# Scores of two steps between the token blocks of a value panel, and a batch of modulation weights loaded before two panels

## The chip, the cores and the metric

The kernel runs on one core of a Trainium2 chip. The core has five engines, each with its own instruction queue, which meet only through semaphores: TensorE (PE, matmuls; its weight loads are shown as PEld), VectorE (DVE), ScalarE (ACT), GpSimd (POOL) and SyncE (SP, which here only issues loads). The metric is the device time of one execution in microseconds (us). All arithmetic is in float32; large products are made from a high and a low part of each operand, in three matmuls.

## The reference

Four layers of a transformer on 512 tokens of width 1024, two with modulation by a vector c, two without. Cut to what the change touches:

```python
def layer_ab(x, c, ...):                      # layer 0
    sh_m, sc_m, g_m, sh_f, sc_f, g_f = jnp.split(silu(c) @ mod_w + mod_b, 6)
    h = rmsnorm(x, norm_mix) * (1.0 + sc_m) + sh_m
    (a_gate, a_x, q, kc, vc, ks, vs, kw, vw, gts) = _split(h @ w_in, IN0_SIZES)
    y_a = rg_lru(causal_conv(a_x), ...) * gelu(a_gate)
    y_b = nsa_mixer(q, kc, vc, ks, vs, kw, vw, sigmoid(gts), ...)   # attention, run 0
    x = x + g_m * (concatenate([y_a, y_b]) @ w_out)
    ...
# layer 1: dsa_mixer (attention over the best 128 keys, run 1)
# layer 2: no softmax attention
# layer 3:
    q, k, v = rotary(qkv[0]), rotary(qkv[1]), qkv[2]
    o = dilated_attention(q, k, v)            # run 2
# in each run, for every head and block of 128 queries:
    s = q @ k.T * scale;  p = softmax(where(mask, s, -inf));  o = p @ v
```

## The kernel before

**Panels.** Weights come from memory as 378 panels of 1024 x 128 (0.5 MB), through a ring of four slots (RING). SP loads a panel into `raw` (L553), ACT rounds it to its high part `w_hi` (split_hi, L1197), POOL subtracts to get the low part `w_lo` (split_lo, L597), and PE multiplies (L662 to L664), into PSUM bank p % 4 for panel p. ACT or DVE then copies the bank away, which counts `bank_free` up. A slot is split anew when PE is done with it. Two panels of values at a time are done by token_panels instead: tokens are the rows of the output then, in QB = 4 blocks of 128 tokens, 24 matmuls of 256 columns each; DVE copies the result out (copy_tokens, L1583 or L1586).

**Modulation.** The first sixteen columns of the modulation come as four batches of 2 MB (`first_mods`, load_first, L562). SP's queue is: columns, x, batch 0, panels 0 to 2, batches 1 to 3, panel 3, then the rest. Of a batch DVE sums three quarters by weight (sum_first, L1858 and L1865) and PE does one quarter and the sums over partitions (first_batch, L672 and L676). first_h(n) on DVE then makes blocks 2n and 2n+1 of h (L1950 to L1965), for which it needs the norm's root: ACT squares x, POOL and PE add, ACT splits panels 0 to 2 and only then takes the root (L1342), DVE takes its reciprocal (invert_root, L1604) in the middle of batch 1's sum, PE spreads it over a bank (spread, L784). PE's panels 0 to 2 run over blocks 0 to 3 of h, then wait for blocks 4 to 7.

**Attention.** Each of the three runs has N_PAIR = 32 steps; a step is a block i of 128 queries and a pair of heads (b = 0, 1), and blocks alternate, 512 keys, 128 keys, 512, 128 and so on at first. Step n goes: scores on PE into two banks (L837), mask and minimum on DVE (masked, L1773), exponentials and sums on ACT (L1283), the reciprocal on DVE (invert, L1783; in run 0 times a gate, L1788), the weights on POOL (weights, L614), transposes on PE (turn, L847), copies to SBUF on ACT and DVE, values on PE (L866). PE issues scores up to SCORES_AHEAD = 3 steps ahead. Steps 0 (banks 4 and 5) differ from the others, which go round banks 0, 1, 6 (run 0) or 0, 1, 6, 7. From n = 2 on, scores wait for `masked_ready` of the step that last had the bank.

Runs 0 and 2 are EARLY: their scores 0 are issued ahead of the last value panel (last_panels: in run 0 panels P_VS, P_VW = 16, 17; in run 2 the panels before P_OUT3), and masks, exponentials, inverse and weights of step 0 are placed beside that panel in the other engines' queues. In run 0 scores 0 stand behind a wait for the key of the windows (kwT, L1364), which ACT copies late because of the recurrence's decays (lru_decays). DVE, behind the token copy of run 0, does two products of the recurrence (recurrence_gated, L2010, two inputs in SBUF), in steps 0 and 1 of its attention loop; POOL splits panels 20 and 21 in the same time.

The order of everything is that in which the code is written, per engine; no scheduler moves it.

Of the kernel before, what the change touches and what calls it, by code (L numbers as in the profile page):

```python
# [131 lines left out]
def build(nc, A):  # L132
    with ExitStack() as ctx:
# [356 lines left out]
        EARLY = (0, 2)  # L490
# [46 lines left out]
        SCORE_BANKS = ((0, 1, 6), (0, 1, 6, 7), (0, 1, 6, 7))  # L537
        PROB_SLOT = (0, 2, 3, 1)

        def score_bank(run, n, b):  # L540

            own = SCORE_BANKS[run]
            return bank[4 + b] if n == 0 else bank[own[(2 * n + b - 2) % len(own)]]
# [4 lines left out]
        def _(sp_):  # L548
# [18 lines left out]
            for p in range(3):  # L567
                load_raw(p)
            for n in range(1, BATCHES):
                load_first(n)  # L570
# [22 lines left out]
        def _(pool):  # L593
# [23 lines left out]
            def attention(run):  # L617

                for n in range(1 if run in EARLY else 0, N_PAIR):
                    weights(run, n)  # L620
                    if run == 0 and n in (8, 9, 10, 11):
                        recurrence_low(n - 8)
# [11 lines left out]
            weights(0, 0)  # L634
            split_from(P_OUT0 + 2, 2)
# [17 lines left out]
            weights(2, 0)  # L653
            split_from(P_OUT3 + 2, 2)
# [5 lines left out]
        def _(pe):  # L660
# [56 lines left out]
            def token_panels(p):  # L717
# [11 lines left out]
                m.then_inc(panel_done, 2)  # L729
# [98 lines left out]
            def attention(run, p_out, last_panels=None):  # L828
                pairs_, at = (PAIRS0, PAIRS1, PAIRS1)[run], N_PAIR * run

                def scores(n):

                    if n >= 2:
# [51 lines left out]
                scores(0)  # L885
                if last_panels is not None:
                    last_panels()
                for n in range(1, SCORES_AHEAD):
# [134 lines left out]
            def last_panels():  # L1023
                token_panels(P_VS)
# [4 lines left out]
            pe.wait_ge(bank_free, P_VS)  # L1029
            pe.wait_ge(cpt_copied, 2)  # L1030
# [143 lines left out]
            def last_panels():  # L1174
                token_panels(P_OUT3 - 2)
# [10 lines left out]
        def _(act):  # L1186
# [99 lines left out]
            def attention(run):  # L1286
# [26 lines left out]
                for n in range(N_PAIR):  # L1313
                    if n >= SCORES_AHEAD:
                        copy_even(n - SCORES_AHEAD)
                    if n or run not in EARLY:
# [75 lines left out]
            for p in range(P_OUT0):  # L1392
# [35 lines left out]
                if p == P_VS:  # L1428
                    exponentials(0, 0)
                split_hi(p + RING)  # L1430
# [117 lines left out]
            for p in range(P_V3, P_OUT3):  # L1548
                if p == P_OUT3 - 2:
                    exponentials(2, 0)  # L1550
                split_hi(p + RING)
# [12 lines left out]
        def _(dve):  # L1564
# [226 lines left out]
            def attention(run, beside=None, times=0):  # L1791
# [20 lines left out]
                early = 1 if run in EARLY else 0  # L1812
# [158 lines left out]
            sum_first(1, lambda: invert_root(0))  # L1971
# [117 lines left out]
            for p in range(P_OUT0):  # L2089
# [22 lines left out]
                elif p == P_VW:  # L2112
                    invert(0, 0)
                    dve.wait_ge(bank_free, P_VS)
# [259 lines left out]
            for p in range(P_V3 + 2, P_OUT3, 2):  # L2374
                if p == P_OUT3 - 2:
                    masked(2, 0, 0)
                    masked(2, 0, 1)
                    invert(2, 0)
                copy_tokens(p, v3t, P * (p - P_V3), root[:, QB:2 * QB])
# [146 lines left out]
```

## Time and profile before

| | us |
|---|---|
| three timed runs | 2465.38, 2467.26, 2467.51 (median 2467.26) |
| the profiled execution | 2463.97 |
| its span on the core | 2462.2 |
| PE busy | 2385.1, 97% of the span |
| DVE, ACT, POOL busy | 1299.1 (53%), 944.3 (38%), 1083.4 (44%) |
| PE's waits in all at L837 (scores) for masks | 9.6, three times |

The profile is of one execution. Its rows give the start of an instruction or of a merged group from the span's start, its duration, and in brackets how long its engine had been idle and who ended that. PE is the engine that is busy nearly always, so its idle stretches are what there is to win. A busy PE isn't always at its peak: its granted clock has two levels, 1.00 (2.4 GHz) and 0.50 (1.2 GHz), and the same matmul takes about twice as long at the lower one.

### The profile page before, as it was taken

What the parts mean: (1) busy time and instruction counts of PE and PEld (TensorE: products, weight loads), DVE (VectorE), ACT (ScalarE), POOL (GpSimd) and SP (SyncE); (2) the same over time, 40 slices, a digit from 0 to 9 for tenths busy, and PEclk for the clock granted to TensorE, in tenths of its full rate; (3) what the DMA queues carried; (4) which work ended last, traced back from release to release, by engine and by line L of the source; (5) the groups of instructions that cost most, each with busy time, mean ns of one, the idle gap of its engine ahead of it and who ended that gap; (6) DMA issues with size and microseconds to landing.
All of it is one profiled execution on the core that took longest, in us unless ns stands there. A gap on an engine that the chain in (4) does not pass through costs nothing.

```text
span 2462.2 us, 34882 instructions
## 1 busy us (share of the span) xinstructions
PE 2385.1 (97%) x11957; PEld 1932.4 (78%) x11957; DVE 1299.1 (53%) x2334; ACT 944.3 (38%) x1538; POOL 1083.4 (44%) x513
## 2 busy tenths in 40 slices
PE   7989999999999899999999989999999999999998
PEld 6776778888876577888888768888888967888887
DVE  6777554443248753111137976455467564645455
ACT  3458332222333743322234544322246374422222
POOL 2336334344433543443445834444454454344433
PEclk9999989999999899999999999999999999999999
DMA  7531335554222012222222213222232201232222
GB/s 309 193 129 53 129 137 180 195 176 146 104 79 78 26 69 82 97 95 94 102 94 94 70 66 121 103 86 103 94 112 97 94 24 60 86 106 92 101 94 77
DMA packets 64195, 261.52 MB, mean 106 GB/s; under 512 B 7248, under 2 KB 7760, under 8 KB 57936
## 3 DMA queue, kind: packets, MB, share of 16 engines
q1 hardware_dynamic: 61056, 251.00, 28.5%
q10 hardware_dynamic: 3024, 8.98, 1.0%
q8 instruction: 73, 1.20, 0.2%
q14 instruction: 42, 0.34, 0.0%
HBM read 257.86 MB, written 2.10 MB: 106 GB/s over the span
## 4 chain that ended last, share of the span: by engine, by line
PE 83%; DVE 7%; issue 4%; POOL 1%; DVEq 1%; DMA 1%; ACT 1%; POOLq 1%; SPq 0%; ACTq 0%
PE bank L662 25%; PE bank L664 25%; PE bank L663 25%; PE bank L847 2%; PE bank L837 2%; PE bank L866 2%; POOL w_lo L597 1%; DVE acc L1596 1%; DVE top L2172 1%; DVEq L2175 1%; DMA first_mods<-in_first 1%; DVE bank L1865 1%; POOLq L651 1%; DVE bank L2222 1%; DVE iacc L2161 1%
## 5 line engine op out<-in xcount | busy, mean ns | idle before, releaser
L597 POOL TENSOR_TENSOR w_lo<-raw,w_hi 128x1024 fp32r<-128x1024 f32 x378 | 917.1, 2434 | 1243.8 <-ACT w_hi L1197 1242.4
L662 PE MATMUL bank<-h_hi,w_hi 128*128 128x512 f32 x1760 | 697.8, 396 | 12.8 <-DVE h_lo L1643 7.8
L664 PE MATMUL bank<-h_hi,w_lo 128*128 128x512 f32 x1760 | 690.3, 392 | 0.0
L663 PE MATMUL bank<-h_lo,w_hi 128*128 128x512 f32 x1760 | 690.2, 392 | 0.0
L1197 ACT ACTIVATE w_hi<-raw 128x1024 fp32r<-128x1024 f32 x378 | 392.5, 1051 | 431.9 <-PE bank L664 428.9
L662 PE MATMUL bank<-g_hi,w_hi 128*128 128x512 f32 x1072 | 418.5, 390 | 0.0
L664 PE MATMUL bank<-g_hi,w_lo 128*128 128x512 f32 x1072 | 417.2, 389 | 0.0
L663 PE MATMUL bank<-g_lo,w_hi 128*128 128x512 f32 x1072 | 417.1, 389 | 0.0
L662 PEld LDWEIGHTS bank<-h_hi,w_hi 128*128 128x128 f32 x1760 | 333.9, 190 | 90.5 <-DVE h_lo L1643 8.7
L664 PEld LDWEIGHTS bank<-h_hi,w_lo 128*128 128x128 f32 x1760 | 333.5, 189 | 71.1
L663 PEld LDWEIGHTS bank<-h_lo,w_hi 128*128 128x128 f32 x1760 | 334.2, 190 | 68.6 <-issue 0.5
L664 PEld LDWEIGHTS bank<-g_hi,w_lo 128*128 128x128 f32 x1072 | 201.2, 188 | 42.3
L662 PEld LDWEIGHTS bank<-g_hi,w_hi 128*128 128x128 f32 x1072 | 201.2, 188 | 41.6 <-issue 0.2
L663 PEld LDWEIGHTS bank<-g_lo,w_hi 128*128 128x128 f32 x1072 | 201.3, 188 | 41.4
L1733 DVE TENSOR_TENSOR prod<-silu,bank 128x512 f32<-128x512 f32 x44 | 30.3, 688 | 303.1 <-PE bank L664 302.8
L614 POOL TENSOR_TENSOR prob<-prob,stat 128x1024 f32<-128x1024 f32 (+1 forms) x96 | 120.1, 1254 | 94.6 <-DVE stat L1783 57.2
L1262 ACT ACTIVATE g_hi<-prod 128x512 f32 x66 | 41.7, 633 | 300.3 <-DVE prod L1733 197.3
L1659 DVE SCALAR_TENSOR_TENSOR x<-bank,plain,x 128x512 f32<-128x512 f32 x64 | 47.6, 748 | 156.9 <-PE bank L664 156.8
L1865 DVE SCALAR_TENSOR_TENSOR bank<-modraw,csil,bank 128x256 f32<-128x256 f32 x222 | 108.5, 489 | 16.9 <-issue 0.4
L1283 ACT ACTIVATE prob<-prob,stat 128x512 f32<-128x512 f32 (+1 forms) x192 | 106.7, 558 | 24.0 <-DVE stat L1773 23.4
L1659 DVE SCALAR_TENSOR_TENSOR x<-bank,modv,x 128x512 f32<-128x512 f32 x64 | 47.3, 748 | 119.2 <-PE bank L664 118.3
L1773 DVE CUSTOM_DVE_ANT_0 prob<-bank,mask 128x512 f32<-128x512 f32 (+1 forms) x192 | 90.1, 485 | 30.7 <-PE bank L837 27.2
(296 smaller groups left out, 2525.0 us busy)
## 6 DMA issues: line engine op xcount, KB each, us to landing
raw<-in_panels SPq DMA_DIRECT2D x378, 512.0 KB, 3.4
modraw<-in_pairs SPq DMA_DIRECT2D x40, 1024.0 KB, 5.6
first_mods<-in_first SPq DMA_DIRECT2D x4, 2048.0 KB, 22.0
x<-in_x SPq DMA_DIRECT2D x1, 2048.0 KB, 8.2
w<-in_w ACTq DMA_DIRECT2D x1, 2048.0 KB, 8.4
out<-yout ACTq DMA_DIRECT2D x8, 256.0 KB, 2.2
mask<-in_causal ACTq DMA_DIRECT2D x1, 1024.0 KB, 5.0
mask<-in_dilated ACTq DMA_DIRECT2D x1, 1024.0 KB, 7.1
```

The costliest lines, as they stand in the source:

```text
L597: pool.tensor_tensor(w_lo[:, slot, :], raw[:, slot, :], w_hi[:, slot, :].bitcast(F32), ALU.subtract)\
L614: pool.tensor_tensor(both, both, stat[:, 2, u:u + 2].rearrange("p (b o) -> p b o", o=1) .broadcast_to((P, 2, w)), ALU.mult).then_inc(weigh ...
L662: pe.matmul(out, w_h, m_h, start=start, stop=False)
L663: pe.matmul(out, w_h, m_l, start=False, stop=False)
L664: return pe.matmul(out, w_l, m_h, start=False, stop=stop)
L837: pe.matmul(score_bank(run, n, b)[:, 0:w], q_of(run, pairs_[n], b), k_of(run, pairs_[n], b), start=True, stop=True).then_inc(score_ready, 1)
L847: m = pe.transpose(bank[2 + b][:, P * j:P * j + P], prob[:, PROB_SLOT[n % PROB_STEPS], b, P * j:P * j + P], ident[:, :])
L1197: act.activation(w_hi[:, slot, :], raw[:, slot, :], ACT.Copy).then_inc(hi_ready, 1)
L1283: act.activation(row, row, ACT.Exp, bias=stat[:, 0, u % 64:u % 64 + 1], scale=-1.0, accum_out=stat[:, 1, u % 64:u % 64 + 1]).then_inc(exp_ ...
L1659: dve.scalar_tensor_tensor(out=x[:, n, :], in0=bank[p % RING][:, :], scalar=scale_by, in1=x[:, n, :], op0=MUL, op1=ADD).then_inc(bank_free, 1)
L1773: dve.tensor_tensor_reduce(row_of(n, b, w), score_bank(run, n, b)[:, 0:w], mask[:, i, 0:w], -SCALE, HIGHEST, ADD, ALU.min, stat[:, 0, u % ...
L1865: m = dve.scalar_tensor_tensor(out=part if k < KB - 1 else to, in0=w[:, :, k, :], scalar=csil[:, k:k + 1], in1=part, op0=MUL, op1=ADD)
```

## The change

- SP's queue at the start: columns, x, batch 0, panel 0, batch 1, panels 1 and 2, batches 2 and 3, panel 3.
- DVE takes the reciprocal of the first root before it begins batch 1's sum; it stood in the middle of that sum.
- In runs 0 and 2 token_panels takes a function `beside`, called behind each of the four blocks of tokens of the last value panel: behind block 0 it issues scores 0, behind block 2 scores 1. The waits for the key and for run 0's cpT move from before the attention into scores 0.
- Scores 1 use banks 4 and 5 as scores 0 do, in all three runs, and wait for both masks of step 0. Steps from 2 on have the banks that they had; scores 2 no longer wait for a mask.
- DVE, ACT and POOL treat step 1 of runs 0 and 2 as step 0 was treated: mask, exponentials, inverse and weights stand ahead of the token copy (DVE), of the split of panel 20 (ACT) and of the splits of panels 20 and 21 (POOL); in run 2 likewise.

```diff
-        EARLY = (0, 2)
+        EARLY = (2, 0, 2)
...
-        SCORE_BANKS = ((0, 1, 6), (0, 1, 6, 7), (0, 1, 6, 7))
+        SCORE_BANKS = ((6, 0, 1), (6, 7, 0, 1), (6, 7, 0, 1))
...
-            return bank[4 + b] if n == 0 else bank[own[(2 * n + b - 2) % len(own)]]
+            return bank[4 + b] if n < 2 else bank[own[(2 * n + b - 4) % len(own)]]
...
             load_first(0)
-            for p in range(3):
+            load_raw(0)
+            load_first(1)
+            for p in range(1, 3):
                 load_raw(p)
-            for n in range(1, BATCHES):
+            for n in range(2, BATCHES):
                 load_first(n)
...
             weights(0, 0)
+            weights(0, 1)
             split_from(P_OUT0 + 2, 2)
...
-            def token_panels(p):
+            def token_panels(p, beside=None):
...
-                m.then_inc(panel_done, 2)
+                    if j == QB - 1:
+                        m.then_inc(panel_done, 2)
+                    if beside is not None:
+                        beside(j)
...
                 def scores(n):
 
-                    if n >= 2:
+                    if run == 0 and n == 0:
+                        pe.wait_ge(bank_free, P_VS)
+                        pe.wait_ge(cpt_copied, 2)
+                    if n == 1:
+                        pe.wait_ge(masked_ready, 2 * at + 2)
+                    elif n >= 3:
                         pe.wait_ge(masked_ready, 2 * (at + n) + 2 - len(SCORE_BANKS[run]))
...
-                scores(0)
                 if last_panels is not None:
-                    last_panels()
-                for n in range(1, SCORES_AHEAD):
+                    last_panels(lambda j: scores(j // 2) if j in (0, 2) else None)
+                for n in range(EARLY[run], SCORES_AHEAD):
                     scores(n)
...
                 if p == P_VS:
                     exponentials(0, 0)
+                    exponentials(0, 1)
...
             sum_first(0)
-            sum_first(1, lambda: invert_root(0))
+            invert_root(0)
+            sum_first(1)
             first_h(0)
...
                 elif p == P_VW:
+                    dve.drain()
+                    for b in range(2):
+                        masked(0, 1, b)
                     invert(0, 0)
+                    invert(0, 1)
                     dve.wait_ge(bank_free, P_VS)
                     copy_tokens(P_VS, vtok0, 0)
```

The same lines for run 2 (weights, exponentials, masks, inverse) are left out.

VectorE at the start, in the order of its queue, before (bank is where the running sum lies, first_mods_80 is batch 1, the row with x3 stands for three instructions):

```order
L1865 SCALAR_TENSOR_TENSOR modsum<-first_mods_79,csil,bank 128x384
L1858 TENSOR_SCALAR bank<-first_mods_80,csil 128x384
L1865 SCALAR_TENSOR_TENSOR bank<-first_mods_80,csil,bank 128x384 x3
L1604 RECIPROCAL root<-root 128x4
L1865 SCALAR_TENSOR_TENSOR bank<-first_mods_80,csil,bank 128x384 x3
L1865 SCALAR_TENSOR_TENSOR modsum<-first_mods_80,csil,bank 128x384
L1950 TENSOR_TENSOR modv<-bank,cols 128x2x2
```

and after:

```order
L1876 SCALAR_TENSOR_TENSOR modsum<-first_mods_79,csil,bank 128x384
L1615 RECIPROCAL root<-root 128x4
L1869 TENSOR_SCALAR bank<-first_mods_80,csil 128x384
L1876 SCALAR_TENSOR_TENSOR bank<-first_mods_80,csil,bank 128x384 x6
L1876 SCALAR_TENSOR_TENSOR modsum<-first_mods_80,csil,bank 128x384
L1961 TENSOR_TENSOR modv<-bank,cols 128x2x2
```

The reciprocal moved from between the fourth and fifth of batch 1's eight instructions to ahead of all of them.

VectorE at the entry of run 0, before (ya is the product of recurrence_gated, L1773 the masks with the bank that they read, vtok the token copy):

```order
L2010 TENSOR_TENSOR ya_97<-ya_97,xc_109 128x512 x2
L1783 RECIPROCAL stat_69<-stat_69 128x2
L1788 TENSOR_TENSOR stat_69<-stat_69,small_76 128x2
L1583 COPY vtok0_107<-bank0 128x512
L1583 COPY vtok0_107<-bank1 128x512
L1843 TENSOR_TENSOR modv_60<-bank7,cols_57 128x20
L2010 TENSOR_TENSOR ya_97<-ya_97,xc_109 128x512
L1773 ISA prob_94,stat_69<-bank0,mask_66 128x128
L1773 ISA stat_69 128x1
L1773 ISA prob_94,stat_69<-bank1,mask_66 128x128
L1773 ISA stat_69 128x1
L2010 TENSOR_TENSOR ya_97<-ya_97,xc_109 128x512
```

and after:

```order
L1784 ISA prob_94,stat_69<-bank4,mask_66 128x128
L1784 ISA stat_69 128x1
L1784 ISA prob_94,stat_69<-bank5,mask_66 128x128
L1784 ISA stat_69 128x1
L1794 RECIPROCAL stat_69<-stat_69 128x2
L1799 TENSOR_TENSOR stat_69<-stat_69,small_76 128x2
L1794 RECIPROCAL stat_69<-stat_69 128x2
L1799 TENSOR_TENSOR stat_69<-stat_69,small_76 128x2
L1594 COPY vtok0_107<-bank0 128x512
L1594 COPY vtok0_107<-bank1 128x512
L1854 TENSOR_TENSOR modv_60<-bank7,cols_57 128x20
L2022 TENSOR_TENSOR ya_97<-ya_97,xc_109 128x512 x2
```

The masks of step 1 and its inverse moved from between and behind the two products to ahead of the token copy, behind the products of chunks 2 and 3; the two products that follow the copy now stand side by side.

TensorE at the same place, before:

```order
L664 MATMUL bank<-w_hi,h_lo 128x256
L683 MATMUL bank<-ones,modsum 128x1 x2
L837 MATMUL bank<-ksT,q_98 128x128 x2
L837 MATMUL bank<-kwT,q_98 128x512 x2
L837 MATMUL bank<-kwT,q_98 128x128 x2
L847 MATMUL bank<-ident,prob 128x128 x8
```

and after:

```order
L668 MATMUL bank<-w_hi,h_lo 128x256
L849 MATMUL bank<-ksT,q_98 128x128 x2
L666 MATMUL bank<-w_hi,h_hi 128x256
...
L668 MATMUL bank<-w_hi,h_lo 128x256
L687 MATMUL bank<-ones,modsum 128x1 x2
L849 MATMUL bank<-kwT,q_98 128x512 x2
L849 MATMUL bank<-kwT,q_98 128x128 x2
L859 MATMUL bank<-ident,prob 128x128 x8
```

Scores 1 (ksT, 128 columns) moved from behind the value panel to ahead of its fourth block.

## Rows read from the trace of the kernel before

**Rows 1.** Order of time, ACT at the start: start us, us, instruction, [idle before, releaser].

```profile
16.98 1.06 ACT L1197 ACTIVATE w_hi<-raw 128x1024 fp32r<-128x1024 f32 x1 [0.23 <-DMA raw<-in_panels]
18.24 1.06 ACT L1197 ACTIVATE w_hi<-raw 128x1024 fp32r<-128x1024 f32 x1 [0.21 <-DMA raw<-in_panels]
...
20.68 0.29 ACT L1342 ACTIVATE root<-bank 128x1 f32<-128x1 f32 x3
```

**Rows 2.** Order of time, DVE at the start.

```profile
23.14 0.62 DVE L1858 TENSOR_SCALAR bank<-first_mods,csil 128x384 f32<-128x384 f32 x1 [3.12 <-DMA first_mods<-in_first]
...
25.76 0.17 DVE L1604 RECIPROCAL root<-root 128x4 f32<-128x4 f32 x1
...
32.58 0.16 DVE L1950 TENSOR_TENSOR modv<-bank,cols 128x4 f32<-128x4 f32 x1 [0.30 <-PE bank L676]
```

**Rows 3.** Order of time, PE at the start, panel 0 taken up again.

```profile
50.16 0.79 PE L662 MATMUL bank<-h_hi,w_hi 128*128 128x512 f32 x1 [1.87 <-DVE h_lo L1965]
```

**Rows 4.** Stretches: from:to, length, PE busy, granted clock, DMA share, GB/s.

```profile
61.00:162.80 101.80, 101.75 (x524) 78.75 (x523) 74.95 (x131) 45.25 (x58) 36.14 (x15) 1.00 0.49 181
...
190.70:191.90 1.20, 1.20 (x8) 0.61 0.00 0
...
820.60:823.10 2.50, 2.50 (x21) 0.50 0.00 0
```

**Rows 5.** Order of time, PE at the entry of run 0.

```profile
165.52 1.13 PE L837 MATMUL bank<-ksT,q 64*128 64x512 f32 x4 [2.77 <-ACT kwT L1364]
...
178.19 0.50 PE L683 MATMUL bank<-ones,modsum 128*128 128x1 f32 x4
179.80 0.49 PE L837 MATMUL bank<-ksT,q 64*128 64x128 f32 x4 [1.11 <-DVE vtok L1583]
182.88 2.08 PE L837 MATMUL bank<-kwT,q 64*128 64x512 f32 x4 [2.59 <-DVE stat L1773]
186.03 0.80 PE L837 MATMUL bank<-kwT,q 64*128 64x128 f32 x4 [1.07 <-DVE stat L1773]
```

**Rows 6.** Order of time, DVE at the entry of run 0.

```profile
176.00 1.48 DVE L2010 TENSOR_TENSOR ya<-ya,xc 128x512 f32<-128x512 f32 x2
...
178.46 1.29 DVE L1583 COPY vtok<-bank 128x512 f32<-128x512 f32 x2 [0.67 <-PE bank L664]
...
180.44 2.17 DVE L2010 TENSOR_TENSOR ya<-ya,xc 128x512 f32<-128x512 f32 x1 [0.61 <-issue]
...
183.12 2.24 DVE L2010 TENSOR_TENSOR ya<-ya,xc 128x512 f32<-128x512 f32 x1
185.29 0.68 DVE L1773 CUSTOM_DVE_ANT_0 prob<-bank,mask 128x512 f32<-128x512 f32 x1
```

**Rows 7.** Order of time, ACT, the last of step 1's exponentials in run 0.

```profile
183.61 0.19 ACT L1283 ACTIVATION_READ_ACCUMULATOR prob<-prob,stat 128x1 f32 x1
```

**Rows 8.** Order of time, POOL at the entry of run 0.

```profile
177.87 1.89 POOL L614 TENSOR_TENSOR prob<-prob,stat 128x1024 f32<-128x1024 f32 x1 [8.98 <-DVE stat L1788]
179.72 2.34 POOL L597 TENSOR_TENSOR w_lo<-raw,w_hi 128x1024 fp32r<-128x1024 f32 x1
182.02 2.80 POOL L597 TENSOR_TENSOR w_lo<-raw,w_hi 128x1024 fp32r<-128x1024 f32 x1
186.98 0.61 POOL L614 TENSOR_TENSOR prob<-prob,stat 128x256 f32<-128x256 f32 x1 [2.16 <-DVE stat L1788]
```

**Rows 9.** Order of time, PE at the entry of run 1.

```profile
813.55 2.50 PE L837 MATMUL bank<-k,q 64*128 64x512 f32 x8 [5.92 <-DVE stat L1773]
816.67 1.97 PE L847 MATMUL bank<-ident,prob 128*128 128x128 f32 x8 [0.61 <-POOL prob L614]
```

**Rows 10.** Order of time, DVE at the entry of run 1, the inverse of step 0.

```profile
814.48 0.17 DVE L1783 RECIPROCAL stat<-stat 128x2 f32<-128x2 f32 x1 [0.55 <-ACT prob L1283]
```

**Rows 11.** Order of time, PE at the entry of run 2.

```profile
1976.02 1.58 PE L837 MATMUL bank<-k,q 64*128 64x128 f32 x12 [1.38 <-DVE v3t L1586]
...
1981.17 0.44 PE L847 MATMUL bank<-ident,prob 128*128 128x128 f32 x2 [1.28 <-POOL prob L614]
```

More of the change, by code:

```diff
@@ L617, in attention @@
             def attention(run):
-                for n in range(1 if run in EARLY else 0, N_PAIR):
+                for n in range(EARLY[run], N_PAIR):
                     weights(run, n)
@@ L653, in _ @@
             weights(2, 0)
+            weights(2, 1)
             split_from(P_OUT3 + 2, 2)
@@ L1022, in _, with last_panels @@
                     compressed_turned()
-            def last_panels():
-                token_panels(P_VS)
+            def last_panels(beside):
+                token_panels(P_VS, beside)
                 with_mods(P_VS)
@@ L1027, in last_panels @@
                 pe.wait_ge(bank_free, P_OUT0)
-            pe.wait_ge(bank_free, P_VS)
-            pe.wait_ge(cpt_copied, 2)
             attention(0, P_OUT0, last_panels)
@@ L1172, in _, with last_panels @@
                 token_panels(p)
-            def last_panels():
-                token_panels(P_OUT3 - 2)
+            def last_panels(beside):
+                token_panels(P_OUT3 - 2, beside)
                 pe.wait_ge(bank_free, P_OUT3)
@@ L1315, in attention @@
                         copy_even(n - SCORES_AHEAD)
-                    if n or run not in EARLY:
+                    if n >= EARLY[run]:
                         exponentials(run, n)
@@ L1550, in _ @@
                     exponentials(2, 0)
+                    exponentials(2, 1)
                 split_hi(p + RING)
@@ L1810, in out_low @@
                                       out_block(run, n, to_hi).bitcast(F32), SUB).then_inc(ot_lo, 1)
-                early = 1 if run in EARLY else 0
+                early = EARLY[run]
                 for n in range(N_PAIR):
@@ L2375, in _ @@
                 if p == P_OUT3 - 2:
-                    masked(2, 0, 0)
-                    masked(2, 0, 1)
+                    for n in range(2):
+                        for b in range(2):
+                            masked(2, n, b)
                     invert(2, 0)
+                    invert(2, 1)
                 copy_tokens(p, v3t, P * (p - P_V3), root[:, QB:2 * QB])
```

## Prediction

> **What bounds the kernel now.** The page says that TensorE (PE) is busy nearly throughout, so an edit pays only if it shortens a stretch in which PE waits, and it costs if it makes a new one. The diff touches four such places: the start, and the entry of each of the three attentions (runs 0, 1, 2). I then read the waits of PE and, engine by engine, the order of time around each place.
>
> At the start PE's panel 0 stops half way and waits 1.87 us for h_lo from VectorE (DVE) [rows 3]. DVE has no slack there: it waits 3.12 us for the second modulation batch, takes it up at 23.14, and from then on is idle only 0.30 us [rows 2] until it releases PE at 50.16. Behind the start, from 61.0 to 162.8, PE is busy for 101.75 of 101.80 us [rows 4]. So a shift of DVE at the start becomes a shift of everything, one for one.
>
> At the entry of run 0 PE waits four times: 2.77, 1.11, 2.59 and 1.07 us [rows 5]. Run 1 has one wait, 5.92 us for the first masked scores, and 0.61 us for the first weights [rows 9]. Run 2 has 1.38 us for the copy of the value panel and 1.28 us for weights from GpSimd (POOL) [rows 11].
>
> **Part 1, the start.** The batch is put ahead of panels 1 and 2 on SP's queue, and DVE takes the reciprocal of the first root before the second batch's sum, no longer in its middle. Bytes in order: before, panel 2 landed at 18.24 and the batch behind it (2 MB) at 23.14, so 4.9 us for 2 MB and 1.2 us for a panel of 0.5 MB [rows 1, 2]. Now the batch lands near 18.24 - 2 x 1.2 + 4.9 = 20.7, and panel 2 near 23.1, since the same bytes come in ahead of it. DVE would be free for the batch at 20.02, so this alone would bring 2.4 us. But the reciprocal now stands in front of the sum, and it needs the root. ScalarE (ACT) makes the root behind its split of panel 2: the split, a table load and four roots, in all from 18.24 to 20.97 [rows 1], 2.7 us. With panel 2 at 23.1 the root is done at 25.85, the reciprocal at 26.05, and the sum starts at 26.1 instead of 23.14: 2.96 later. The sum is free of the reciprocal, which took a slot of 0.1 to 0.2 in its middle, and the idle 0.30 us is swallowed [rows 2], which leaves **+2.6 us**, for h_lo and so for PE. PE has room meanwhile: its 1.87 us of waiting stays about as long. Bounds: 0 if panels 1 and 2 still landed by 18.24; +2.9 if the 0.30 isn't swallowed.
>
> **Part 2, run 0.** PE now begins the value panel at once (162.75), and scores 0 come behind its first block of tokens. From 166.6 to 178.2 the four blocks take 11.6 us [rows 5], 2.9 each, so scores 0 stand at 165.65, when their key (the wait that ended at 165.52) is ready. The 2.77 us are hidden. Scores 1 come after the third block, and PE is through at 176.2 instead of 178.7. What is late next is DVE, not PE:
> - Up to 177.4, where its gated products of chunks 2 and 3 end [rows 6], DVE goes as before (scores 0 end within 0.15 us of where they did).
> - Now it masks scores 1, 0.5 us (182.61 to 183.12 in [rows 6]), and inverts step 0 (0.4 us, what lies between 177.4 and the 0.67 of idling at 178.46), so POOL gets its factor at 178.45 rather than 177.87 [rows 8]. ACT's exponentials of step 1 end 1.2 us after the mask started ([rows 6, 7]: 182.6 to 183.80), at 178.75. DVE waits for them, inverts step 1 (0.4) and copies the tokens from 179.25 instead of 178.46 [rows 6].
> - PE's next scores waited until 1.34 us after that copy began [rows 5, 6]: now 180.6. PE is idle for 4.4 us, and scores 2 run from 180.6.
> - POOL does the weights of step 0 (1.85), now those of step 1 too (0.6), and then splits two panels; the split starts at 178.45 + 1.85 + 0.6 = 180.9 instead of 179.72 [rows 8].
> - DVE reaches the two gated products (L2010) at 181.2, and they fall under those splits again.
>
> How those products behave decides the sum. Alone, 1.48 us for two would be 0.7 each [rows 6]; under the splits they show 2.17 and 2.24. The first ended 0.6 us after the first split (which ended at 182.0), and the second split took 2.80 and ended at 184.82, the second product 0.5 us later [rows 6, 8]. They stand until a split is over. So the second product ends 0.5 us after the second split, and that is 1.2 us later than before: masks of scores 2 at 186.5 instead of 185.29, scores 3 at 187.25 instead of 186.03, **+1.2 us**; the rest of the run follows in the same order. The Trainium skill states this too ("SBUF — State Buffer", section "SBUF: two separate sides": a VectorE instruction with two SBUF inputs and a GpSimd instruction that reads SBUF lock each other out for a whole instruction); the trace agrees, by the 0.5 us. Were the two merely slowed, each at its 2.2 us, the masks would stand at 185.75 and the term would be +0.5.
>
> Bounds: +0.5, and +2 if the token copy, which ran beside POOL's weights in 1.29 [rows 6, 8], were held by them; a case below gives less than zero.
>
> **Part 3, run 1.** It has no value panel to lie beside, but the table of banks changes for it too: scores 1 now use the banks of scores 0 and wait until both are masked. In the row of 813.55, scores 2 and 3 went out together [rows 9]; now scores 1, 2 and 3 go out there. Masks 1 wait for scores 1, whose two halves take 0.8 us at this clock (scores 3 at 186.03 in [rows 5] are the same shape), so the inverse that stood at 814.48 [rows 10] moves to 814.75, and the first transposes from 816.67 to 817.0: **+0.3 us**. Bounds: +0.7 (all of the 0.8 shows), and -1.5, if PE, now without its 0.61 us of idling, gets the high clock back earlier than at 823.1 [rows 4].
>
> **Part 4, run 2.** PE has one step of scores (0.4 us) less behind the panel and one more ahead of it; it waits for the token copy either way, and scores 2 stand where they did. Weights 1 are made ahead of the two splits, so the 1.28 us at 1981.17 go [rows 11]. But weights 2 now stand behind the same splits: those start 0.4 later (the panel ends 0.4 later) and 0.6 of weights is gone from behind them. So transposes 2 come 0.2 earlier than before: **-0.2 us**. Bounds: -1.3 and +0.4.
>
> Wait tests and a few drains are the rest: no row shows one over 0.1 us.
>
> **The sum:** 2.6 + 1.2 + 0.3 - 0.2 = +3.9 us. The profiled execution took 2463.97 us, so it would take 2467.9. The timed runs stand at a median of 2467.26 (3.3 above it), so I forecast 2471.2, by +3.9 from that median.
>
> **Rivals.**
> - *The loads land out of order.* If panels 1 and 2 come in beside the batch, the root is there at 21 as before, and the batch not before 23.1. Then the start gives 0 and the sum is +1.3: 2468.6. For it: all share 16 engines. Against: panels 1 and 2 landed 1.26 us apart, and the batch, four times as large, 4.9 us behind them [rows 1, 2]. The Trainium skill ("DMA: Bandwidth & Descriptors", "Queues, rings and completion order") says that completion isn't strictly first in, first out per issuing engine; the rows here look like it is. 8%.
> - *The early batch pays.* The sum starts at 20.7 and the reciprocal costs nothing: -2.4 at the start, -1.1 in all, 2466.2. Against it stands ACT's order, in which the root is behind panel 2. 4%.
> - *A product slips in ahead of the split.* In run 0 DVE asks at 181.2 and POOL at 180.9. If DVE is 0.3 us sooner, the first product takes 0.7, only one split stands before the second, and the masks stand at 184.8: -0.5 instead of +1.2; in all +2.2, 2469.5. 14%.
> - *Slower: the low clock stays longer in run 0.* Behind the wait at 182.88 scores of one size took 2.08 us, against 1.13 at 165.52 [rows 5]: the clock was at its lower level, 0.50 or 1.2 GHz, and came back inside 190.7 to 191.9 [rows 4], 5.4 us after PE took up work at 186.03. In run 1 it took from 813.55 to behind 823.1, 9.6 us, with one gap of 0.61 us [rows 4, 9]. After the change PE idles for 4.4 us, works for 2 and idles for 4.5 more. If the return takes 9.6 us from 187.25, there are 4.2 us more at half speed, 2.1 us lost: +6.0, 2473.3. It decides from a return after 194.7. 14%.
>
> **How the numbers follow.** The forecast has 60%, the rivals 8, 4, 14 and 14. About 0.2%, 4.9 us, is what a measurement of this kernel can tell from no change. The forecast's own terms reach from about +2.5 to +5, and the runs before spread over 2.1 us, so I put 12 of its 60 above +4.9; with the clock's 14 that makes 26% slower. Faster by 4.9 us has no case, 2% for what I don't see; 72% within. The range 2466.5 to 2474.0 takes in every case but the second rival's lower part, with a margin for the spread of the runs.
>
> **What would show it.** Start: the second sum's first row on DVE at 26.1 behind the reciprocal (at 20.7 the second rival, at 23.1 the first), panel 2's split on ACT at 23.1, PE's panel 0 resumed at 52.8. Run 0, times less the shift of 2.6: no wait of PE before scores 0, token copy at 179.25, split at 180.9, scores 3 at 187.25, clock back near 192.6. Run 1: PE's transposes 0.3 us later. Run 2: no wait for weights 1, one of 1.3 us for weights 2. I am wrong if the root isn't last at the start, or if the three entries together differ from +1.3 by more than 1.5 us.

## The result and the profile after

| | before | changed |
|---|---|---|
| median of the timed runs (lowest to highest), us | 2465.53 (2462.84 to 2467.51), 12 runs | 2470.04 (2465.75 to 2471.18), 12 runs |
| ratio to before | | 1.0016, interval 1.0008 to 1.0023 |
| the profiled execution, us | 2463.97 | 2466.16 |
| its span, us | 2462.2 | 2464.4 |

The change costs 0.16%, 3.9 us by the ratio and 4.5 by the medians: slower, and just inside what was called no change. The forecast was +3.9.

The two profiled executions are only 2.2 us apart. Executions of one kernel differ, much of it by how much of the time TensorE was granted its high clock: over the span, the mean clock goes from 0.981 to 0.985. With one straight line for all kernels of this study, an execution is 1.2 us shorter for each 0.001 of mean granted clock, and single executions then scatter by 0.7 us around their kernel's line. The profiled execution of the changed kernel was one of two at 0.985; five of the twelve were at 0.981, with a mean of 2470.9. The profiled execution of before was at 0.985 too, so the mean clock doesn't explain the small difference of the pair: by the line they would be 3.6 us apart, and before's lies 1.0 us above the line while the other's lies 0.4 us below it, which is within the scatter. At an equal clock the change costs 3.6 us; the twelve executions of before that were timed beside it have no clock on record, so this figure rests on the 93 timed later. The table of experiments below gives it for each kernel too, worked out in the same way.

**The start, after.** ACT's order of time (start us, us, instruction, idle before and releaser), to be held beside [rows 1]:

```profile
15.94 1.06 ACT L1206 ACTIVATE w_hi<-raw 128x1024 fp32r<-128x1024 f32 x1 [1.93 <-DMA raw<-in_panels]
22.12 1.06 ACT L1206 ACTIVATE w_hi<-raw 128x1024 fp32r<-128x1024 f32 x1 [5.12 <-DMA raw<-in_panels]
23.39 1.06 ACT L1206 ACTIVATE w_hi<-raw 128x1024 fp32r<-128x1024 f32 x1 [0.21 <-DMA raw<-in_panels]
24.46 1.28 ACT L1351 ACT_TABLE_LOAD   x1
...
25.82 0.29 ACT L1351 ACTIVATE root<-bank 128x1 f32<-128x1 f32 x3
```

Panels 1 and 2 land behind the batch, at 22.12 and 23.39, and the root is made behind both splits. DVE's order of time, beside [rows 2]:

```profile
26.15 0.18 DVE L1615 RECIPROCAL root<-root 128x4 f32<-128x4 f32 x1 [5.89 <-ACT root L1351]
26.25 0.59 DVE L1869 TENSOR_SCALAR bank<-first_mods,csil 128x384 f32<-128x384 f32 x1
27.35 4.11 DVE L1876 SCALAR_TENSOR_TENSOR bank<-first_mods,csil,bank 128x384 f32<-128x384 f32 x6 [0.51 <-issue]
...
35.79 0.16 DVE L1961 TENSOR_TENSOR modv<-bank,cols 128x4 f32<-128x4 f32 x1
```

DVE idles 5.89 us for the root where it had idled 3.12 for the batch, and begins the sum at 26.25. PE, beside [rows 3], takes up panel 0 at 53.37 and not at 50.16, with the whole start 0.24 us later from the first batch on (14.74 against 14.50):

```profile
53.37 0.80 PE L666 MATMUL bank<-h_hi,w_hi 128*128 128x512 f32 x1 [1.45 <-DVE h_lo L1976]
```

**Run 0, after.** The shift of the start is in these times: it stands at +2.7 us here. The 0.5 us between this and the 3.21 at panel 0 came back by the clock: it was low around the resumed panel and rose 4.9 us after it in before (50.16 to about 55.0) and 3.8 us after it here (53.37 to about 57.2). PE, beside [rows 5]:

```profile
168.37 1.13 PE L849 MATMUL bank<-ksT,q 64*128 64x512 f32 x4
...
175.38 0.49 PE L849 MATMUL bank<-ksT,q 64*128 64x128 f32 x4
...
184.39 2.08 PE L849 MATMUL bank<-kwT,q 64*128 64x512 f32 x4 [5.13 <-DVE vtok L1594]
190.09 0.80 PE L849 MATMUL bank<-kwT,q 64*128 64x128 f32 x4 [3.62 <-DVE stat L1784]
```

Scores 0 and 1 lie between the token blocks, with no wait: the 2.77 us are gone. Two waits of 5.13 and 3.62 us stand in the place of 1.11, 2.59 and 1.07. DVE and POOL, beside [rows 6] and [rows 8]:

```profile
180.99 0.16 DVE L1799 TENSOR_TENSOR stat<-stat,small 128x2 f32<-128x2 f32 x1
181.57 0.17 DVE L1794 RECIPROCAL stat<-stat 128x2 f32<-128x2 f32 x1 [0.42 <-ACT prob L1292]
181.81 1.33 DVE L1799 TENSOR_TENSOR stat<-stat,small 128x2 f32<-128x2 f32 x1
183.06 1.28 DVE L1594 COPY vtok<-bank 128x512 f32<-128x512 f32 x2
...
184.56 4.86 DVE L2022 TENSOR_TENSOR ya<-ya,xc 128x512 f32<-128x512 f32 x2
189.35 0.68 DVE L1784 CUSTOM_DVE_ANT_0 prob<-bank,mask 128x512 f32<-128x512 f32 x1
```

```profile
181.23 2.60 POOL L616 TENSOR_TENSOR prob<-prob,stat 128x1024 f32<-128x1024 f32 x2 [9.62 <-DVE stat L1799]
183.79 5.09 POOL L599 TENSOR_TENSOR w_lo<-raw,w_hi 128x1024 fp32r<-128x1024 f32 x2
```

The stretch in which the clock came back, at 193.7:

```profile
193.00:194.00 1.00, 1.00 (x4) 0.22 (x3) 0.00 (x0) 1.00 (x5) 1.00 (x1) 0.66 0.00 0
```

POOL's two splits end at 188.88 and DVE's two gated products 0.5 us later, as they did before. One thing is new: the little product of step 1's inverse (128x2), 0.16 us for step 0, takes 1.33 us for step 1. It began beside POOL's weights of step 0.

**Runs 1 and 2, after.** PE, beside [rows 9] and [rows 11]:

```profile
815.29 2.93 PE L849 MATMUL bank<-k,q 64*128 64x128 f32 x12 [5.89 <-DVE stat L1784]
818.74 1.09 PE L859 MATMUL bank<-ident,prob 128*128 128x128 f32 x8 [0.51 <-POOL prob L616]
...
1977.80 1.35 PE L849 MATMUL bank<-k,q 64*128 64x512 f32 x8 [1.38 <-DVE v3t L1597]
...
1981.98 0.41 PE L859 MATMUL bank<-ident,prob 128*128 128x128 f32 x2 [0.53 <-ACT probT L1304]
...
1984.24 1.09 PE L859 MATMUL bank<-ident,prob 128*128 128x128 f32 x8 [0.41 <-POOL prob L616]
```

The first transposes of run 1 take 1.09 us at once and not 1.97: here the clock was already back. The profile's stretches show it (columns as in [rows 4], after PE the other engines):

```profile
817.00:818.40 1.40, 1.23 (x6) 0.42 (x4) 1.09 (x4) 0.34 (x2) 1.40 (x1) 0.53 0.00 0
818.40:820.30 1.90, 1.56 (x11) 1.16 (x12) 1.71 (x9) 1.74 (x5) 0.90 (x2) 1.00 0.00 0
```

Before, it came back at 823.1 [rows 4]. This took the profiled execution from +2.1 us at these transposes to -0.1 at the run's last ones. Later it fell back again, to +1.2 ahead of run 2 and +2.2 at the end, so it is one of several such swings in this pair and not a gain that stayed.

### The profile page after: what moved, and what is told of

Its sections match the earlier page's. It is cut to its first block, busy times and chain, and to the rows that moved or that the text cites. A ratio compares the mean times of both kernels' runs of the same rounds, so it can differ in the third digit from the quotient of the medians.

```text
span 2464.4 us, 34883 instructions
## 1 busy us (share of the span) xinstructions
PE 2384.8 (97%) x11957; PEld 1932.7 (78%) x11957; DVE 1301.8 (53%) x2334; ACT 942.9 (38%) x1538; POOL 1082.9 (44%) x513
## 4 chain that ended last, share of the span: by engine, by line
PE 84%; DVE 7%; issue 3%; DVEq 2%; POOL 1%; ACT 1%; DMA 1%; POOLq 1%; SPq 0%; ACTq 0%
PE bank L666 25%; PE bank L668 25%; PE bank L667 25%; PE bank L849 2%; PE bank L859 2%; PE bank L878 2%; DVEq L2191 1%; DVE top L2188 1%; POOL w_lo L599 1%; DMA raw<-in_panels 1%; DVE acc L1607 1%; POOLq L654 1%; DVE bank L2238 1%; DVE iacc L2177 1%; DVE bank L1876 1%
```

## The experiments

Theory: three of the change's four places cost what the sum says; the start is the dear one, since the root moved behind the batch and the reciprocal stands in front of the sum; in run 0 POOL's splits hold DVE's gated products. Rival for the start: the loads alone do it. Rival for run 0: the products are slow by themselves, or hiding the wait pays. Rival for run 1: it gives back 2 us by its clock, as the profiled execution looks.

Each kernel was timed against before on the same chip. "Equal clock" is the difference to before by the line described above (93 executions of before, 11 of each other, 12 of the changed kernel). The line has two limits. It takes out what an edit does to the clock itself, so where that is the question (q0, r1) the ratio is what counts; and the executions of before, taken by round, lie up to 0.4 us apart on it, so a figure is good to about 0.4 us. The last two columns are read in each profiled execution, less before's: PE's panel 0 taken up again (50.16 before), and by how much the shift grows over run 0, from the end of the stretch ahead of it (162.75 before) to the first matmul of the projection behind it (258.02 before). They are those of one execution, clock and all.

| kernel | median us | ratio (interval) | equal clock | PE at 50.16 | run 0 |
|---|---|---|---|---|---|
| changed | 2470.04 | 1.0016 (1.0008 to 1.0023) | +3.6 | +3.21 | +0.5 |
| s1, the start alone | 2467.85 | 1.0010 (1.0001 to 1.0019) | +2.5 | +2.94 | -0.1 |
| s2, the loads alone | 2467.23 | 1.0002 (0.9993 to 1.0011) | +0.3 | +0.19 | +1.7 |
| s3, start with the root ahead | 2463.17 | 0.9989 (0.9980 to 0.9998) | -2.3 | -1.81 | +3.0 |
| a1, the three entries alone | 2466.03 | 1.0001 (0.9991 to 1.0010) | +0.6 | -0.14 | +1.0 |
| q0, run 0's entry alone | 2464.44 | 0.9999 (0.9990 to 1.0008) | -0.1 | +0.12 | +0.9 |
| r1, run 1's entry alone | 2466.20 | 1.0005 (0.9996 to 1.0014) | +0.4 | +0.07 | +1.5 |
| r3, before with products ahead | 2462.42 | 0.9991 (0.9982 to 1.0000) | -1.8 | -0.29 | -1.4 |
| r2, a1 with products ahead | 2464.88 | 0.9998 (0.9989 to 1.0007) | +0.4 | -0.14 | -0.2 |
| best1, changed, root and products ahead | 2463.57 | 0.9995 (0.9986 to 1.0004) | -1.3 | -1.60 | -0.1 |
| best2, before with start, root, products ahead | 2461.53 | 0.9985 (0.9976 to 0.9994) | -3.4 | -1.98 | -0.7 |
| best3, best1 with inverse 1 behind the copy | 2460.53 | 0.9985 (0.9976 to 0.9994) | -3.2 | -1.89 | -1.3 |

### The start: s1, s2, s3

s2 is before with the new order of loads alone; s1 has the reciprocal ahead of the sum too; s3 is s1 with ACT's root ahead of its splits. The three edits:

```
             load_first(0)
-            for p in range(3):
+            load_raw(0)
+            load_first(1)
+            for p in range(1, 3):
                 load_raw(p)
...
-            sum_first(1, lambda: invert_root(0))
+            invert_root(0)
+            sum_first(1)
...
-            for p in range(3):
-                split_hi(p)
+            split_hi(0)
             act.wait_ge(sums_ready, 1)
             for j in range(QB):
                 m = act.activation(root[:, j:j + 1], ...)
             m.then_inc(root_ready, 1)
+            for p in range(1, 3):
+                split_hi(p)
```

> The kernel before with the new load order and the reciprocal ahead of the sum, the attentions as before. Theory (the reciprocal waits for a root that is made behind panel 2): the second sum starts on DVE near 26.1, PE takes panel 0 up again 2.6 to 3 us later than at 50.16, and PE's marks near 76, 105 and 142 stand 2.7 later, as in the changed kernel: time +2.7 us. Rival (most of the change's loss is made in the attentions, and the start is absorbed later): marks back to +0 by 300, time within 1 us.

> The kernel before with the new load order only; the reciprocal stays in the middle of the sum. Theory: the sum starts near 20.7, stands still in its middle until the root at 25.9, and ends at 28.8 as before (28.7): PE's marks within 0.3 us, time within 0.5 us. Rival (it is the later landing of panels 1 and 2, not the reciprocal's place, that costs): +2 us or more.

> The new load order, the reciprocal ahead of the sum, and ACT's root ahead of its splits of panels 1 and 2, so that the root waits for no load behind panel 0. Theory: root near 21, the sum starts near 21.1 instead of 23.14, PE's marks stand 1.9 us earlier, time -1.9 us. Rival (DVE would be late for another reason, such as PE's part of batch 1): 0 to -0.5.

s1 shows the change's start, +2.9 at PE and +2.5 at an equal clock. In s2 the batch lands at 20.63 and DVE takes it up at once, but half way it meets the reciprocal and waits for the root (DVE, order of time):

```profile
20.63 0.62 DVE L1860 TENSOR_SCALAR bank<-first_mods,csil 128x384 f32<-128x384 f32 x1 [0.57 <-DMA first_mods<-in_first]
21.33 2.02 DVE L1867 SCALAR_TENSOR_TENSOR bank<-first_mods,csil,bank 128x384 f32<-128x384 f32 x3
25.94 0.18 DVE L1606 RECIPROCAL root<-root 128x4 f32<-128x4 f32 x1 [2.59 <-ACT root L1344]
26.21 2.01 DVE L1867 SCALAR_TENSOR_TENSOR bank<-first_mods,csil,bank 128x384 f32<-128x384 f32 x3
```

Half of the sum lies in the wait, and s2 comes out level with before. So the late root bounds both, and where the reciprocal stands decides whether the sum's first half is beside it or behind it. In s3 ACT makes the root before it waits for panel 1, and DVE gets all (first ACT, then DVE):

```profile
19.08 0.36 ACT L1343 ACTIVATE root<-bank 128x1 f32<-128x1 f32 x4 [1.10 <-PE bank L913]
21.81 1.06 ACT L1199 ACTIVATE w_hi<-raw 128x1024 fp32r<-128x1024 f32 x1 [2.37 <-DMA raw<-in_panels]
```

```profile
20.05 0.18 DVE L1607 RECIPROCAL root<-root 128x4 f32<-128x4 f32 x1
20.53 0.62 DVE L1861 TENSOR_SCALAR bank<-first_mods,csil 128x384 f32<-128x384 f32 x1 [0.30 <-DMA first_mods<-in_first]
```

The sum starts at 20.53, PE's panel 0 is taken up 1.8 us earlier than before and 5.0 earlier than in the changed kernel, and the kernel is faster than before by 0.11%. The sum starts 2.6 us earlier than before and PE only 1.8. Lost on the way are 0.51 us in a gap behind the sum's first instruction, and 0.64 at a little product behind the sum (gains, 128x2, two inputs in SBUF), which takes 0.80 us at 26.82 where it took 0.16 in before, and ends at 27.62 with POOL's two splits (22.95 to 27.61); the reciprocal's slot in the sum and the idle 0.30 us are saved. The early load was a good edit with one order left as it was.

### Run 0 and run 1 alone: a1, q0, r1

a1 is the changed kernel with the first two of these edits taken back. q0 is a1 with runs 1 and 2 as before; r1 is before with the banks and the wait of run 1 alone. q0 against the changed kernel (the start, the waits and run 2's lines, which go back to before, are left out), then r1 against before:

```
-        EARLY = (2, 0, 2)
+        EARLY = (2, 0, 1)
...
-        SCORE_BANKS = ((6, 0, 1), (6, 7, 0, 1), (6, 7, 0, 1))
+        SCORE_BANKS = ((6, 0, 1), (0, 1, 6, 7), (0, 1, 6, 7))
...
+            first = 2 if run == 0 else 1
+            return bank[4 + b] if n < first else bank[own[(2 * (n - first) + b) % len(own)]]
```

```
-            return bank[4 + b] if n == 0 else bank[own[(2 * n + b - 2) % len(own)]]
+            return bank[4 + b] if n < (2 if run == 1 else 1) else bank[own[...]]
...
-                    if n >= 2:
+                    if n == 1 and run == 1:
+                        pe.wait_ge(masked_ready, 2 * at + 2)
+                    elif n >= (3 if run == 1 else 2):
```

> The changed kernel with the start as before. Theory: +1.3 us by the forecast's terms (run 0 +1.2, run 1 +0.3, run 2 -0.2); by the trace of the changed kernel run 0 +0.5, run 2 0 to -0.1, and run 1 anything from +0.3 to -2.5 as the clock comes back late or early; time between -2 and +1.3. Rival (the entries are what costs): +3 us or more.

> Before, with the entry of run 0 alone as in the change (start, run 1 and run 2 as before). My theory of the trace of the change: PE's wait of 2.77 us before scores 0 is gone, yet scores 3 come later than their 186.03 of before, because DVE copies the tokens later and the two gated products still stand until POOL's second split is over; the recorded sum has +1.2 us for it, and the trace of the change gave +1.4 at scores 3 (190.09, less the start's 2.7). So: split near 181.1, scores 3 near 187.4, whole kernel +1.2 us (2 at most). A theory in which hiding the wait pays gives -1 us or less. The look at the entries alone gave +1.64 at the first transposes and +1.25 from the third on.

> Before, with run 1's banks and wait alone as in the change. The recorded term is +0.3 us at the first transposes (from 816.67), since scores 1 go out behind the first masks and not ahead of them; bounds +0.7 and -1.5, the latter if PE has the high clock back sooner. The trace of the change lost nothing and won 2.2 us here (from +1.98 to -0.09), because the clock rose at 818.4 and not at 823.0. If the edit does that, this kernel shows the same, and it is some 2 us faster than before; if the moment at which the clock rises wanders by itself, transposes stand 0 to 0.3 us later and the time is within 0.5 us of before.

The entries together cost 0.6 us at an equal clock, and no interval tells them from nothing. In run 0 a1 and q0 show what the changed kernel shows: the copy late, DVE's products of 4.86 us under the splits, and a shift that grows by 0.9 to 1.0 us. But the timed q0 is at -0.2 us by its ratio, with an interval from -2.5 to +2.0, and at -0.1 at an equal clock. A possible reason is in the profiled executions of the kernels that keep the wait of 2.77 us before scores 0. In before, s1 and best2 the four matmuls behind it took 1.13 us, and from there to the small matmuls at the panel's end it was 12.7 us. In four others the clock fell about this wait. PE in s3:

```profile
163.87 2.08 PE L839 MATMUL bank<-ksT,q 64*128 64x512 f32 x4 [2.77 <-ACT kwT L1367]
```

and its stretches:

```profile
164.00:166.00 2.00, 2.00 (x5) 0.50 (x5) 0.00 (x0) 1.98 (x2) 1.16 (x1) 0.50 0.88 274
166.00:168.00 2.00, 2.00 (x10) 2.00 (x11) 1.81 (x5) 1.99 (x5) 1.20 (x1) 0.50 0.60 250
168.00:170.00 2.00, 2.00 (x12) 2.00 (x12) 1.77 (x5) 1.97 (x3) 0.00 (x0) 0.58 0.84 252
170.00:172.00 2.00, 2.00 (x19) 2.00 (x18) 1.83 (x4) 1.10 (x4) 0.00 (x0) 1.00 0.03 10
```

There the same piece took 15.3 us (s3, r1), 15.4 (s2) and 14.2 (r3). In the six kernels whose scores lie between the blocks the clock stayed at 1.00 throughout. So the wait cost, beside its 2.77 us, 1.5 to 2.7 us in four executions of seven, and the profiled execution of before, on which the forecast rests, was one of the three without. Taking the wait away gives that back where it happens. How often it happens in timed runs no row shows; that it evens out run 0's loss there fits q0's ratio, whose interval holds +0.9 just as well, so it isn't shown. The equal clock can't tell here: it takes such a gain out.

In r1 the first transposes come 3.45 us after the second row of scores starts (814.35 to 817.80), as in the changed kernel (815.29 to 818.74), and 3.12 before (813.55 to 816.67): +0.33. The clock came back in r1 only at 823.7, as in before. How long it took from that row of PE on, in the profiled executions: without the edit of run 1 9.5 (before), 9.4 (s2), 9.1 (s3), 7.2 (best2), 7.0 (r3), 6.2 (s1) and 6.2 us (q0); with it 9.5 (a1), 9.3 (r1), 9.6 (best1), and 3.1 in the changed kernel, r2 and best3. So the 2.2 us that the changed kernel's trace gave back here are no fixed gain of the edit: r1 has the edit and doesn't have them. That 3.1 us was seen in three of six with the edit and in none of seven without suggests that it makes the early return possible; r1's ratio, whose interval starts at -1.0 us, leaves no room for a fixed gain of 2 us. Whether the edit brings a smaller one stays open.

### What holds DVE in run 0: r3, r2, best3

r3 is before with the two gated products moved from behind POOL's splits to ahead of the token copy; r2 is the same on a1:

```
-                    if run == 0 and n in (0, 1):
-                        recurrence_gated(n)
...
                     recurrence_gated(2)
                     recurrence_gated(3)
+                    recurrence_gated(0)
+                    recurrence_gated(1)
```

> Before, with DVE's gated products of chunks 0 and 1 in run 0 done right behind those of chunks 2 and 3 (at 177 us), so that they no longer stand behind POOL's two splits of panels. If these splits hold the products, as the prediction says (4.4 us for two under them, 1.48 us for two without), DVE gains about 2.9 us behind the splits and spends 1.5 ahead of the token copy, of which its idle 0.67 us hides a part: token copy 0.8 later (179.3), masks of scores 2 near 183.2 instead of 185.29, scores 3 near 184 instead of 186.03, so -2 us. If the products are slow by themselves, 2.2 each wherever they stand, the copy comes 3.7 us later and the whole is +1 us or worse.

> The three entries of the change with the old start, and the gated products ahead of the token copy. Against the entries alone (trace +1.25 us in run 0 from the third transposes on): without the products behind the splits run 0 comes 1.7 us sooner, at -0.4 to -0.5 against before, and the time is 0 to 1 us below before. If the splits are not what the third masks waited for, it stays at +1.25.

DVE in r3:

```profile
174.76 3.05 DVE L2008 TENSOR_TENSOR ya<-ya,xc 128x512 f32<-128x512 f32 x4
...
182.46 0.69 DVE L1773 CUSTOM_DVE_ANT_0 prob<-bank,mask 128x512 f32<-128x512 f32 x1 [1.00 <-PE bank L837]
```

Four products in 3.05 us, 0.76 each, where two under the splits took 4.4 (before) and 4.86 (changed). Masks 2 stand at 182.46 and not at 185.29; 1.2 us of this were there by scores 0. The kernel is 1.8 us faster at an equal clock, 2.2 by the ratio. On a1 the move took run 0's growth from +1.0 to -0.2 in the trace; in the times 0.2 us of it showed at an equal clock and 0.7 by the ratios, neither clear of noise. It pays less here because nothing hides the products ahead: counted from scores 0, the token copy stands 1.7 us later in r2 (181.31 less 164.91) than in a1 (180.65 less 165.95), and PE waits 6.83 us for it and not 5.13. DVE's little product is held on top of that in both, for 1.33 us in a1 and 1.47 in r2 (179.91). best1 has it as well (178.62), and best3 moves it: the inverse of step 1 behind the copy, and POOL's weights of step 1 behind its splits.

```
                     invert(0, 0)
-                    invert(0, 1)
                     dve.wait_ge(bank_free, P_VS)
                     copy_tokens(P_VS, vtok0, 0)
+                    invert(0, 1)
...
             weights(0, 0)
-            weights(0, 1)
             split_from(P_OUT0 + 2, 2)
+            weights(0, 1)
```

> The changed kernel with ACT's root and the gated products ahead, as in the last of the runs before, and besides with DVE's inverse of step 1 behind the token copy, and POOL's weights of step 1 behind its two splits, as they stand in before. The inverse's product of 128x2 took 1.47 us there, beside POOL's weights of step 0, where its twin took 0.16. If the lock is what holds it, the token copy starts at 178.4 and not at 180.0, PE has scores 2 at 179.8 and not at 181.3, and the whole is 1.5 us faster than that run. If it is not, the copy waits or is slow beside POOL's weights, and the time is that of the run before.

DVE and then POOL in best3:

```profile
177.52 1.29 DVE L1595 COPY vtok<-bank 128x512 f32<-128x512 f32 x2
178.73 0.15 DVE L1795 RECIPROCAL stat<-stat 128x2 f32<-128x2 f32 x1
178.96 0.61 DVE L1800 TENSOR_TENSOR stat<-stat,small 128x2 f32<-128x2 f32 x1
```

```profile
177.66 1.89 POOL L616 TENSOR_TENSOR prob<-prob,stat 128x1024 f32<-128x1024 f32 x1 [11.34 <-DVE stat L1800]
```

The copy stands at 177.52 (180.01 in best1, whose scores 0 are 0.55 later, so 1.9 us are won). Of these, 1.3 are the time that the little product was held, and the rest is DVE's wait for ACT's exponentials and its own work on the inverse, which went behind the copy too. The copy runs beside POOL's weights in 1.29 us and isn't held. The little product behind it is again not over before POOL's weights end at 179.55. Against best1 the kernel is 1.9 us faster at an equal clock.

### Both kernels beaten: best1, best2

> The changed kernel with ACT's root ahead of its splits of panels 1 and 2, and with DVE's gated products of chunks 0 and 1 ahead of the token copy. By the terms: start -1.8 (as its own run showed at PE's panel 0) against +3.2 in the change; run 0 about 2 to 3.5 us sooner than in the change (the products are out from under the splits, masks of scores 2 near 183 instead of 187.6 less the start's shift); run 1 and run 2 as in the change. Together -3 to -4 us against before, 2461 to 2463 us, and the fastest of the kernels here. If the cover of run 0 doesn't move (the products are not what masks 2 waited for), it is at -0.5 to -1.

> Before, with the batch ahead, the reciprocal ahead of the second sum, ACT's root ahead of its splits of panels 1 and 2, and the gated products of chunks 0 and 1 ahead of the token copy; no other entry changed. If the two gains stand in places that don't touch each other, they add up: 1.8 us at PE's panel 0, and 1.4 to 1.6 at run 0, together 3.2 to 3.4 us by the traces and 4.9 by the timed ratios of the two alone (0.9989 and 0.9991), so 2460 to 2462 us: the fastest here. If the wait of 2.8 us before scores 0, which is still there, lets the clock fall within the value panel, as in two of the kernels before, some 2.4 us of it are lost again and it is level with the products alone.

best1 (changed, with s3's root and the products ahead) fell short of its -3 to -4 us, at -1.3: ahead of its token copy stand the two products, the wait for the exponentials of step 1 and the held little product, and moving the last two (best3) brought 1.9 us at an equal clock. best2 leaves out the entries and has both gains: -3.4 us, 0.15% faster than before, as the sum of s3 (-2.3) and r3 (-1.8) would nearly have it. best2 and best3 can't be told apart, and both are faster than before and the changed kernel.

## Why the prediction was right

The time came out at 2470.04 against 2471.2, and the difference to before at +3.9 (ratio) against +3.9. That these two agree to a tenth is luck: the ratio's interval goes from +2.0 to +5.7 us, the equal clock gives +3.6, and the parts alone measured 2.5 and 0.6 where the forecast had 2.6 and 1.3. The time was 1.2 us off, mostly because the three runs that it was built on had a median of 2467.26 and the twelve have 2465.53. By its steps:

- **The start, +2.6: right, +2.5 at an equal clock** (s1), +2.7 in the changed kernel's trace by scores 0. The steps are there one by one: batch out of the way (20.63 in s2, forecast 20.7), panel 2 split at 23.39 (23.1), sum from 26.25 (26.1). PE resumed at 53.37, not 52.8: I let the 0.30 us of idling be swallowed and the sum be shorter without the reciprocal, but a gap of 0.51 us, of which the profile only says "issue", stands behind the sum's first instruction in s1, s3 and the changed kernel. That makes +2.94 in s1; in the changed kernel's profiled execution +3.21, past the bound of +2.9. It was not carried on one for one as the prediction had it: the clock gave 0.5 us back before run 0.
- **Both rivals of the start fell.** The loads landed in order, with panel 2 behind the batch in each trace. The early batch paid nothing until ACT's order was changed; s3 shows the -1.8 us that it then pays, of the 2.4 that the rival gave it; the held product of gains is 0.64 of the difference.
- **Run 0, +1.2: the mechanism right, the size too large.** Less 2.7, the split came at 181.1 (forecast 180.9), masks 2 at 186.65 (186.5) and scores 3 at 187.4 (187.25). The Trainium skill's rule ("SBUF — State Buffer", "SBUF: two separate sides": a VectorE instruction with two SBUF inputs and a GpSimd instruction that reads SBUF lock each other out) was right for the products, and it was read too narrowly: it holds for the inverse's little product as well, which took 1.33 us, to the end of POOL's weights, where the sum had 0.2. The token copy was 1.1 us later than forecast (180.4 less the shift, 179.25); by the order of the rows it cost nothing, since DVE would have stood at the splits anyway. From scores 3 on +1.4 became +0.5 by the end of the run: the clock came back at 193.7, 3.6 us after scores 3 began, not 5.6 as before (the prediction read 5.4), and 1.6 us ahead of the forecast (192.6 and 2.7). The timed q0 can't confirm the size (-0.2 by its ratio, within 2 us). The prediction also took PE's wait of 2.77 us at its length alone, from an execution of before in which the clock had stayed up through it.
- **The rival of the product that slips in ahead** fell: DVE reached the products 0.8 us after POOL's split began. **The slower rival**, the low clock for longer, fell too: it would have decided from 197.4 (194.7 and the shift), 3.7 us later than the clock came back.
- **Run 1, +0.3: right** (+0.33 in r1 and in the changed kernel, +0.4 at an equal clock). The early return of the clock, its lower bound, was there in the profiled execution and isn't a fixed part of the edit.
- **Run 2, -0.2: nil.** The shift is +1.19 ahead of it and +1.22 behind it (+3.03 and +3.06 in a1). The wait for weights 1 went, and PE waited 0.15 us for masks, 0.53 for ACT's copy of the transposes and 0.41 for weights 2, in place of the 1.3 that I had put there.
- **The sum** holds as parts: 2.5 for the start and 0.6 for the entries make 3.1, against 3.6 for the whole. The scatter of 0.7 us per execution leaves 0.2 for each kernel's mean, and rounds differ by up to 0.4, so the remaining 0.5 can't be given to a cause.

## What to carry over

When a load is put ahead of others, follow the queue of every engine that waits for the ones put back: here a root that needed none of them stood behind two splits, and made a gain of 1.8 us a loss of 2.5. A wait of the matmul engine costs more than its length where the clock falls with it, which it did here in four of seven executions; so one profile doesn't price it, and a difference of 2 us between two profiled executions calls for a comparison of the granted clock, stretch by stretch. And where VectorE's instruction with two SBUF inputs began under a GpSimd tensor_tensor, it stood until that was over, whatever its own size: look for the small ones too.

## What the runs showed of the hardware

- A VectorE product of 128x2 took 0.16 us free, and 1.33 (changed kernel), 1.47 (r2, best1), 0.61 (best3) and 0.83 us (r3) where it began under a GpSimd tensor_tensor; it ended within 0.03 us of that instruction each time. A copy out of PSUM beside the same GpSimd work took 1.27 to 1.29, in every kernel.
- After an idle stretch of 2.77 us, matmuls of one shape took 1.13 us in three executions and 2.08 in three others, in the same place of the program. In the seventh (r3) they took 1.13 as well and the clock fell about 1 us after they began.
- In run 1 the granted clock came back 3.1 to 9.6 us after PE had taken up work, in nearly the same program. Over a whole execution the mean clock varies from 0.981 to 0.985 (once 0.986, in best3), and that goes with some 5 us between executions of the changed kernel.
